# Hybrid conformer/attention/MoE block: the wide expert passes turn their result on VectorE instead of TensorE, with strided weights

## The reference, cut to what matters

```python
def clamped_swiglu_expert(xb, w1, b1, w2, b2):
    h = xb @ w1 + b1
    x_glu = jnp.minimum(h[..., :D_FF], SWIGLU_LIMIT)
    x_lin = jnp.clip(h[..., D_FF:], -SWIGLU_LIMIT, SWIGLU_LIMIT)
    act = x_glu * jax.nn.sigmoid(SWIGLU_ALPHA * x_glu) * (x_lin + 1.0)
    return act @ w2 + b2

# v = rms_norm(h, norm2_g); gates = softmax over the 4 largest router logits
y_assign = ys[dest].reshape(T, TOP_K, D)
y = h + jnp.einsum("tk,tkd->td", gates, y_assign)
```

## Time and profile before

| | |
|---|---|
| median of 3 runs | 1993.06 us (1991.5 to 1994.81) |
| the profiled execution | 1994.85 us |
| its span, first to last instruction | 1993.1 us |
| granted TensorE clock, mean | 0.992 |
| narrow passes, wide passes | 18, 14 |

### The profile page before, as it was taken

How to read it: one execution, slowest core, us unless ns; L and a number is a source line. 1 busy time by engine, 2 the same in 40 slices (tenths; PEclk the granted TensorE clock), 3 DMA queues, 4 the chain that set the end, 5 groups by cost and what they waited for, 6 DMA issues and landing times.

```text
span 1993.1 us, 35237 instructions
## 1 busy us (share of the span) xinstructions
PE 1925.4 (97%) x12983; PEld 1589.3 (80%) x12984; DVE 1010.1 (51%) x2627; ACT 449.9 (23%) x983; POOL 415.6 (21%) x410
## 2 busy tenths in 40 slices
PE   5999989989999999999999999999999999999996
PEld 3545545457888877888887888999999999999996
DVE  2989973354555545555554555444444444443332
ACT  3166565111111111111111111222222211211111
POOL 3111100011222222222232222222222222221211
PEclk9999999999999999999999999999999999999998
DMA  7000033538999999999999999999888899887651
GB/s 242 1 1 1 6 112 136 186 114 293 349 343 332 352 338 350 351 341 332 351 339 351 351 347 331 313 323 311 303 301 302 304 308 308 298 294 244 223 181 40
DMA packets 237153, 513.21 MB, mean 258 GB/s; under 512 B 11085, under 2 KB 15721, under 8 KB 237104
## 3 DMA queue, kind: packets, MB, share of 16 engines
q1 hardware_dynamic: 215408, 448.89, 62.6%
q0 software_dynamic: 19840, 63.23, 11.9%
q10 hardware_dynamic: 1856, 0.41, 0.1%
HBM read 479.30 MB, written 33.19 MB: 257 GB/s over the span
## 4 chain that ended last, share of the span: by engine, by line
PE 91%; DVE 4%; ACT 2%; issue 1%; DMA 1%; POOL 0%; SPq 0%; ACTq 0%; DVEq 0%; POOLq 0%
PE bank L1175 50%; PE bank L1219 12%; PE bank L1194 12%; PE bank L1392 5%; PE bank L1267 4%; DVE arena L932 2%; PE bank L1303 2%; PE bank L1314 1%; PE bank L1207 1%; PE bank L1553 1%; PE bank L1208 1%; PE bank L1342 1%; DMA arena<-in_x 1%; PE bank L1259 0%; PE bank L1366 0%
## 5 line engine op out<-in xcount | busy, mean ns | idle before, releaser
L1175 PE MATMUL bank<-arena 128*128 128x128 f32 (+5 forms) x8192 | 1000.7, 284 | 6.9 <-issue 6.1
L1175 PEld LDWEIGHTS bank<-arena 128*128 128x128 f32 x8192 | 986.5, 191 | 18.8 <-issue 17.8
L377 POOL DMA_INDIRECT arena<-token_rows,idx_q x256 | 250.1, 977 | 649.0 <-PE bank L1175 589.1
L808 DVE TENSOR_SCALAR arena<-bank,b1c 128x256 f32<-128x256 f32 x256 | 123.4, 482 | 407.2 <-PE bank L1175 407.2
L497 ACT ACTIVATE arena<-arena 128x256 f32<-128x256 f32 x256 | 106.6, 417 | 853.9 <-DVE arena L808 853.9
L1219 PE MATMUL bank<-arena 128*128 128x512 f32 x576 | 250.2, 592 | 0.0
L1194 PE MATMUL bank<-arena 128*128 128x144 f32 (+4 forms) x1792 | 246.8, 293 | 3.0 <-ACT arena L501 2.9
L1194 PEld LDWEIGHTS bank<-arena 128*128 128x128 f32 x1792 | 235.3, 190 | 6.2 <-ACT arena L501 6.2
L383 POOL DMA_INDIRECT out<-arena,idx_cur x64 | 99.4, 1553 | 535.9 <-DVE arena L865 492.1
L1219 PEld LDWEIGHTS bank<-arena 128*128 128x128 f32 x576 | 108.1, 190 | 129.1 <-issue 129.1
L932 DVE SCALAR_TENSOR_TENSOR arena<-arena,cols 128x512 f32<-128x512 f32 (+1 forms) x226 | 182.3, 807 | 12.5 <-ACT arena L592 5.5
(11 more groups left out here) (229 smaller groups left out, 1102.4 us busy)
## 6 DMA issues: line engine op xcount, KB each, us to landing
arena<-in_w SPq DMA_DIRECT2D x192, 2048.0 KB, 12.6
arena<-in_b SPq DMA_DIRECT2D x32, 512.0 KB, 12.7
arena<-in_x SPq DMA_DIRECT2D x16, 512.0 KB, 6.4
token_rows<-arena SPq DMA_DIRECT2D x8, 576.0 KB, 3.2
out<-arena SPq DMA_DIRECT2D x8, 512.0 KB, 6.0
arena<-token_rows,idx_q POOLq DMA_INDIRECT x256
arena<-in_w_in SPq DMA_DIRECT2D x2, 1536.0 KB, 13.1
arena<-in_w_in SPq DMA_DIRECT2D x1, 3072.0 KB, 19.5
```

The lines of the kernel that those rows point to most:

```text
L377: pool.indirect_dma_start(out=gath_q[:, g, :], out_offset=None, in_=quads_d, in_offset=bass.IndirectOffsetOnAxis(ap=idx_q[:, g:g + 1], axis=0)
L808: v.tensor_scalar(g1[:, r, :], bank[r][:, 0:SLOTS], b1c[:, m:m + 1], LIMIT, ALU.add, ALU.min).then_inc(g1_ready, 1)
L1175: last = mm(bank[m % 2][:, side * SLOTS:side * SLOTS + n], w1_sb[:, k, lo:lo + P], xT[:, k, 0:n], start=k == 0, stop=k == KD - 1)
```

## The change

In wide passes the stationary operand of the down projection becomes every eighth column of w2 (a step of 32 bytes), so that partition p of block d holds output column 8p + d. ScalarE adds b2 on the way out of PSUM (from `b2c`, 8 values a partition, a new small DMA in each pass). TensorE's transposes go. VectorE turns each block in 32x32 blocks (`turn_y`), four before the x blocks and four after them. Each partition then holds quarters of tokens; ScalarE multiplies each of 8 groups by its gate and sorts the columns (`weigh_quads`), and GpSimd adds 8 groups of 128 quarter rows (`add_quads`). Gates and indices per quarter are carried along in new small copies. VectorE's program is the same for narrow and wide passes, so it turns blocks and does two L865 in both. A narrow pass sends one add. GpSimd waits for the landing of the adds at the head of the pass. Both halves of w2 are loaded after the whole down projection.

```diff
@@ sync
-                for c in range(2):
-                    sp.wait_ge(y_mm, q * KD + (4 * c + 4 - KD))
+                sp.wait_ge(y_mm, q * KD)
+                for c in range(2):
                     load_w2(sp, c, e)
@@ load_b2
             sp.dma_start(b2_rows, src.to_broadcast([P, D])).then_inc(b2_in, 16)
+            sp.dma_start(b2c[:], src.rearrange("o (p d) -> (o p) d", d=KD)).then_inc(b2c_in, 16)
@@ gpsimd
+        def add_quads(pool, groups):
+            pool.sem_inc(pool_past, 1)
+            for g in groups:
+                pool.indirect_dma_start(out=out_quads,
+                                        out_offset=bass.IndirectOffsetOnAxis(ap=idx_q_cur[:, g:g + 1], axis=0),
+                                        in_=y_quads[:, g, :], in_offset=None, compute_op=ALU.add).then_inc(added, 16)
...
             with pool.Fori(0, n_pass) as q:
+                pool.wait_ge(added, pool.snap(sent, min_val=32, max_val=32 + 128 * QMAX))
+                pool.sem_inc(landed, 1)
                 over = pool.value_load(tabI[0:1, ds(q + TQ, 1)])
                 pool.wait_ge(idx_q_ready, q + 1)
                 for i in range(4):
                     pool.wait_ge(hid_mm, q * 8 + 5 + i)
                     gather_quads(pool, (2 * i, 2 * i + 1))
-                pool.wait_ge(y_ready, q + 1)
-                for i in range(2):
-                    pool.wait_ge(added[i], q * 16 + 16)
-                pool.sem_inc(pool_past, 1)
-                add_rows(pool, 0, ytok[:, 0, :])
                 with pool.If(over < 1):
-                    add_rows(pool, 1, zeros)
+                    pool.wait_ge(y_ready, q + 1)
+                    add_rows(pool)
+                    pool.reg_add(sent, sent, 16)
                 with pool.Else():
-                    add_rows(pool, 1, ytok[:, 1, :])
+                    for i in range(4):
+                        pool.wait_ge(quads_ready, q * 4 + (i + 2))
+                        add_quads(pool, (2 * i, 2 * i + 1))
+                    pool.reg_add(sent, sent, 128)
@@ scalar
             def take_yT(d):
+                if d == 0:
+                    a.wait_ge(b2c_in, q * 16 + 16)
+                    a.wait_ge(turned, q + 1)
                 a.wait_ge(y_mm, q8 + d + 1)
-                a.activation(yT[:, d, :], bank[2 + d % 2][:, 0:SLOTS], ACT.Copy).then_inc(yT_ev, 1)
+                a.activation(yT[:, d, :], bank[2 + d % 2][:, 0:SLOTS], ACT.Identity, bias=b2c[:, d:d + 1]).then_inc(yT_ev, 1)
+            def weigh_quads():
+                a.wait_ge(cur_ready, q + 1)
+                a.wait_ge(turned, q + 2)
+                for g in range(8):
+                    last = a.activation(y_quads[:, g, :].rearrange("p (i d) -> p d i", d=KD),
+                                        y_turned[:, g, :].rearrange("p (d i) -> p d i", d=KD), ACT.Copy,
+                                        scale=gate_q_cur[:, g:g + 1])
+                    if g % 2 == 1:
+                        last.then_inc(quads_ready, 1)
@@ vector
-                if m == 4:
-                    for i in range(2):
-                        v.wait_ge(added[i], q * 16 + 16)
+                if m == 6:
+                    v.wait_ge(landed, q + 1)
                     v.tensor_copy(idx_cur[:], idx_pass[:])
+                    v.tensor_copy(idx_q_cur[:], idx_q_pass[:])
+                    v.tensor_copy(gate_q_cur[:], gate_q_pass[:])
                     link(v.tensor_copy(gate_cur[:], gate_pass[:]))
                     v.sem_inc(cur_ready, 1)
             hidden_b(MT - 1)
+            def turn_y(d):
+                v.wait_ge(yT_ev, q8 + d + 3)
+                return v.transpose(y_turned[:, :, d * 32:(d + 1) * 32], yT[:, d, :].rearrange("p (g r) -> p g r", r=32))
+            v.wait_ge(quads_ready, q * 4 + 1)
+            for d in range(KD // 2):
+                turn_y(d)
             v.wait_ge(quad_in, q * 128 + 128)
             for g in range(8):
                 ins = v.transpose(xT[:, :, g * 32:(g + 1) * 32], gath_q[:, g, 0:D // 4].rearrange("p (k r) -> p k r", k=KD))
...
+            for d in range(KD // 2, KD):
+                last = turn_y(d)
+            last.then_inc(turned, 1)
@@ tensor
                     last = mm(bank[2 + d % 2][:, 0:n],
-                              w2_sb[:, m, d * P:(d + 1) * P], act[:, m, 0:n],
+                              w2_sb[:, m, :].rearrange("p (c d) -> p d c", d=KD)[:, d, :], act[:, m, 0:n],
                               start=m == 0, stop=m == MT - 1)
...
-            for d in range(2, 6):
+            for d in range(2, KD):
                 down(d, range(MT))
-                trans_y(d - 2)
-            down(6, range(MT))
-            down(7, range(MT))
-            for d in range(4, KD):
-                trans_y(d)
@@ tensor, once ahead of the loop
+            pe.wait_ge(spots_ready, 1)
+            for i, src in enumerate((spots, gsel)):
+                last = mm(bank[3][:, 8 * i:8 * i + 8], copies[:], src[:].rearrange("p h g -> p (h g)"), start=True, stop=True)
+            last.then_inc(spread_mm, 1)
```

More of the change, by code:

```diff
@@ L92, in hybrid_block @@
         g2_row = part(140, D)
-        ytok = part(144.5, 2, D)
+        y_quads = part(144.5, 8, D // 4)
+        y_turned = part(164.5, 8, D // 4)
+        ytok = part(172.5, D)
         zeros = part(140, D)[0:2, :]
@@ L193, in hybrid_block @@
         idx_q = sb("idx_q", [P, 8], i32)
+        idx_q_pass = sb("idx_q_pass", [P, 8], i32)
+        idx_q_cur = sb("idx_q_cur", [P, 8], i32)
+        gate_q_pass = sb("gate_q_pass", [P, 8])
+        gate_q_cur = sb("gate_q_cur", [P, 8])
+        b2c = sb("b2c", [P, KD])
         copies = sb("copies", [P, P])
@@ L247, in hybrid_block @@
         y_mm, yT_ev, yt_mm, yt_ev = sem("y_mm"), sem("yT_ev"), sem("yt_mm"), sem("yt_ev")
-        added = [sem(f"added{i}") for i in range(2)]
+        added, landed, turned, quads_ready, b2c_in = (sem(n) for n in (
+            "added", "landed", "turned", "quads_ready", "b2c_in"))
         pool_past = sem("pool_past")
@@ L379, in gather_quads, with add_rows @@
                                         ).then_inc(quad_in, 16)
[L381 to L384, removed]
+        def add_rows(pool):
+            pool.sem_inc(pool_past, 1)
+            pool.indirect_dma_start(out=out2, out_offset=bass.IndirectOffsetOnAxis(ap=idx_cur[:, 0:1], axis=0),
+                                    in_=ytok, in_offset=None, compute_op=ALU.add).then_inc(added, 16)
+        def add_quads(pool, groups):
+            pool.sem_inc(pool_past, 1)
+            for g in groups:
+                pool.indirect_dma_start(out=out_quads,
+                                        out_offset=bass.IndirectOffsetOnAxis(ap=idx_q_cur[:, g:g + 1], axis=0),
+                                        in_=y_quads[:, g, :], in_offset=None, compute_op=ALU.add).then_inc(added, 16)
         @block.gpsimd
@@ L518, in take_rows @@
                     a.wait_ge(cur_ready, q + 1)
-                    for i in range(2):
-                        a.wait_ge(added[i], q * 16 + 16)
-                a.activation(ytok[:, 0, b * HALF:(b + 1) * HALF], bank[4 + b][:], ACT.Copy,
+                a.activation(ytok[:, b * HALF:(b + 1) * HALF], bank[4 + b][:], ACT.Copy,
                              scale=gate_cur[:, 0:1]).then_inc(yt_ev, 1)
-                a.sem_inc(yT_ev, KD // 2)
             with a.If(over < 1):
                 sigmoids()
+                a.sem_inc(yT_ev, KD)
                 take_rows(0)
                 take_rows(1)
+                a.sem_inc(quads_ready, 4)
             with a.Else():
                 sigmoids()
-                for d in range(6):
+                a.sem_inc(yt_mm, 2)
+                a.sem_inc(yt_ev, 2)
+                for d in range(KD):
                     take_yT(d)
-                take_y(0)
-                take_yT(6)
-                take_yT(7)
-                take_y(1)
+                weigh_quads()
         @block.scalar
@@ L857, in dve_pass @@
                                  quad[:].unsqueeze(1).to_broadcast([P, 2, 4]), ALU.mult))
[L858 removed]
+            v.tensor_reduce(gate_pass[:], gsel[:], AX.X, ALU.add)
+            link(v.tensor_copy(gate_q_pass[:], gath_q[:, :, ds(e_next + D // 4, 1)].rearrange("p g o -> p (g o)")))
             v.sem_inc(dve_loop, OWN - own[0])
[L860 removed]
+            for d in range(KD // 2, KD):
+                last = turn_y(d)
+            last.then_inc(turned, 1)
+            q16 = v.snap(q * 16 + 16)
+            v.wait_ge(b2c_in, q16)
+            v.wait_ge(b2_in, q16)
             for b in range(2):
                 v.wait_ge(yt_ev, q * 2 + b + 1)
[L863 to L866 removed]
+                y = ytok[:, b * HALF:(b + 1) * HALF]
+                last = v.scalar_tensor_tensor(y, b2_rows[:, b * HALF:(b + 1) * HALF], gate_cur[:, 0:1], y,
+                                              ALU.mult, ALU.add)
             last.then_inc(y_ready, 1)
@@ L1151, in _ @@
             link(v.tensor_tensor(rank[:], rka[:], rkd[:], ALU.add))
```

(3 more changed lines are left out.)

51 lines of the change are left out of this document (17 added, 34 removed).

## The result

2162.02 us (2160.45 to 2164.24) against 1993.38, medians of four executions each: 1.0847 of before, 95% interval 1.0829 to 1.0866. I had forecast 1972 us with a range of 1963 to 2060, and gave a chance of 0.15 to the case near 2146 that came.

What follows compares the result with a forecast made beforehand. TensorE, busy for 97% of the span, was taken to bound the kernel; -28 for wide passes, +6.7 at the end and +0.5 at the start gave -20.8 us, so 1972 us, range 1963 to 2060.

Steps and rivals of the forecast that it cites:

- the case near 2146: Wide down projection: a stepped weight load taking twice as long, 174 us more in all; chance 0.15.
- I take nothing for the step and keep 79 and 174 us for the range: Wide down projection's weight loads: stepped columns cost nothing; 79 and 174 us more kept as possible prices.
- The VectorE row: VectorE sum of 128 elements 128 bytes apart: 358 ns against 286 adjacent; the 72 ns perhaps a neighbouring GpSimd fill's.
- the doubled load: Wide down projection: a stepped weight load at twice 114.5 ns, 229 ns a record, 174 us more.
- The first rival: Wide down projection: slow stepped load paid in 1792 TensorE records, 2051 or 2146 us; chance 0.35.
- The 13 wide passes with one behind them: TensorE without transposes and the idle gap at pass end: 2.15 us less per wide pass, 28 us over 13.
- The last pass and the tail: After the last wide pass nothing hides the eight adds: end 6.7 us later (3 to 9), landing equal.
- The start: Ahead of the loop two small matmuls wait for four small VectorE steps: 0.5 us more (0 to 1.5).
- VectorE's turns and ScalarE's weighing: Turns of 0.34 us and weighings of about 0.4 us, done some 4 us into the next pass: hidden.
- Adds: GpSimd's eight quarter-row adds, 1.4 us each, ending 15.6 us (12 to 17.4) after the last down matmul: hidden.
- The second rival: Adds after wide passes land too late, TensorE waits 4 us in 13 passes, 2024 us; chance 0.06.
- w2 later: SyncE's queue: both halves of w2 leave after the down projection, hidden at a cost of 0 to 1 us.

Runs made afterwards that it cites:

- the probe: Kernel before plus single VectorE and ScalarE instructions over 256 stepped elements behind the last pass; VectorE sums with steps four and eight took 0.19 us more than one.

## Why the prediction was wrong

**The step that failed** is "I take nothing for the step and keep 79 and 174 us for the range". The step measured 190 us, above the upper of the two bounds: a record of L1240 takes 243 ns, not some 125. Three things went wrong in it. The VectorE row was explained away by a fill that ran beside it; the probe shows such a price without any neighbour, and even a little above the row's. The row was then scaled as a ratio, 1.54 x 114.5 = 176 ns, where the price is a time for each line: the row's own 205 ns for 128 columns was nearer to the 243 measured than 176. And the doubled load, 229 ns, was a round factor, no bound.

The argument before it was right: a load near the record's length shows at once, break-even is at 141 ns, and 1792 records multiply it. The first rival was right in place and mechanism. The Trainium skill (SBUF — State Buffer, section "Door 1: The DMA port swizzle") says that full bandwidth wants at least two accesses to a line of 16 bytes. The trace agrees: with two columns a line the record stays at 128 ns, with one it takes 237. The next sentence there calls a step of up to four float32 free, and here the measurement decides: a step of four costs 237 ns against 128.

**The other terms** are judged by the run with adjacent columns. Forecast for the sum 1972 us, measured 1971.93; that the two agree so closely is luck. The profiled execution of that run spans 1968.8 us against 1993.1, 24.3 less, where the terms had said 20.8, and they differ from it one by one. Against the kernel before, by the starts of the passes in both timelines:
- The 13 wide passes with one behind them are 24.8 us shorter, 1.9 each, where 28 us, 2.15 each, was forecast. The gap at the pass end is gone (L1220 with 0.0 idle against 2.0). But without the transposes in between TensorE waits more within the down projection: L1240 is idle for 9.0 us over all widths, for ScalarE's copies and for `act`, where L1194 was for 2.8. Two of the three passes of width 136 gained only 0.1 and 0.8 us. In them VectorE stood still for 3.7 us ahead of the last block of `act`, for a releaser that the profile calls "remote"; what that is stays open.
- The last pass and the tail are 5.5 us longer; 6.7 was forecast. From the last copy on it is 25.1 us instead of 18.8, 6.3 more. My working has 6.7 + 0.85 = 7.6 there, and two errors in it largely cancel: the eight adds end 17.8 us after the copy starts, not 15.6, and what follows them takes 7.3 us instead of the 10.7 of before, where I had taken the landing as equal.
- The start: the first wide pass begins 5.0 us earlier, and I had forecast 0.5 later. The first expert pass alone begins anywhere from 449.7 to 453.4 us in the traces of both kernels and their variants, so this lies mostly between executions.
- VectorE's turns and ScalarE's weighing: hidden, as said, but with less to spare. A weighing takes 4.34/8 = 0.54 us, not 0.4, and the copy with bias 0.47, not 0.39. In the pass above the weighing ends 5.5 us into the next one, not 4.
- Adds: 1.56 us each, not 1.4, the first 3.1 us after the last copy starts, not 2, so the eight end at 17.9, just past my 17.4. The gathers begin 24.9 us into the pass, inside the 25.5 that cost nothing (25.0 in a pass of width 136 of the run with adjacent columns). The second rival did not come.
- w2 later: no wait of TensorE for a load in a wide or narrow pass.

The chances were wrong in size. A written rule, a row that leaned its way, and a load with no slack stood against an argument that the row might be disturbed; 0.35 for the slow load was too little.

## What to carry to other kernels

Before a stepped operand goes to TensorE, count the 16-byte lines that its columns lie in: at 1.85 to 1.9 ns a line against 0.86 ns for a column that moves (125 ns for 144, 434 for 512), a stationary operand in float32 with a step of two is about free, and one with a step of four or eight nearly doubles a record of 128 to 144 columns. An estimate from the same numbers is that it hides from some 280 moving columns on (243/0.86); the runs show it hidden at 512 and not at 192. If no row shows the price, take the nearest stepped row as a time for each element, not as a ratio, and do not explain it away without a second one. Look also at which of two interleaved blocks ends first: a reordering of two lines gained 7 us, a third of what the whole change gains without its step.

## What the runs showed that I had not expected

- A step costs moving operands too (905 ns instead of 434 for 512 columns). With a step of 16 bytes or more a VectorE sum or product pays some 0.7 ns a column more, a copy 0.4, and a ScalarE copy about 1.0.
- After a wait of 2.15 us of TensorE the granted clock was at 0.50 for some 3.4 us in 12 of 18 equal passes, and stayed at 1.00 in the six others; it cost 1.7 us each time.
- Four matmuls of 32 stationary columns run side by side in 136 ns, but leave TensorE idle for "issue", 41 us over 14 passes.
- A ScalarE copy of 32 partitions takes as long as one of 128 (0.48 us), and may be written to another group of partitions.
